# A two-block transformer kernel: the lower halves of the weight tiles on GpSimd, the key copies on VectorE

## What is computed

```python
x = first_block(x, c, ...)      # per layer: mod = silu(c) @ w_ada + b_ada; h = modulated rmsnorm(x); x += gate * rmsnorm(mixer(h) @ w_out)
for i in range(2):              # second block
    mod = silu(c_2) @ ada_w[i] + ada_b[i]
    h = modulate(rms_norm(x, norm1_g[i]), sh1, sc1)
    y = conformer_conv(h, ...) if i == 0 else hgrn2_mixer(h, ...)
    x = x + g1 * y
    h = modulate(rms_norm(x, norm2_g[i]), sh2, sc2)
    x = x + g2 * (relu(h @ w1) ** 2 @ w2)
return rms_norm(x, final_g)
```

## Time and profile before

| what | value |
|---|---|
| median of 3 runs | 2681.1 us (2674.4 to 2684.4) |
| the profiled execution | 2674.6 us, its span 2672.9 us |
| busy TensorE / VectorE / ScalarE / GpSimd | 2187.3 / 1567.2 / 918.7 / 5.3 us |
| mean granted TensorE clock | 0.91 of full |
| w_lo (L305) on VectorE | 293 instructions, 336.2 us |

### The profile page before, as it was taken

The page is one execution under the profiler, slowest core; times in us unless marked ns, Lnnn a source line. Parts: engine busy times, 40 slices in busy tenths (PEclk is TensorE's granted clock), DMA queues, the critical chain, the costliest instruction groups (busy, mean ns, idle before and its releaser), DMA issues.

```text
span 2672.9 us, 25870 instructions
## 1 busy us (share of the span) xinstructions
PE 2187.3 (82%) x9666; PEld 1641.3 (61%) x9666; DVE 1567.2 (59%) x2744; ACT 918.7 (34%) x1625; POOL 5.3 (0%) x12
## 2 busy tenths in 40 slices
PE   1898994899899665338999998777777778899997
PEld 0665563676566344216888885666666666688885
DVE  4566665666255489964655554666666674433332
ACT  2334442343322321023332233544444443422331
POOL 0000000000000000000000000000000000000000
PEclk9998997899898887669999999888888889999998
DMA  6321113333122211101555551011101111232221
GB/s 261 135 101 60 34 64 122 110 126 111 63 70 88 87 32 48 32 16 56 189 179 183 181 173 64 24 39 33 40 32 40 40 32 57 70 95 95 95 95 48
DMA packets 65723, 228.44 MB, mean 85 GB/s; under 512 B 6976, under 2 KB 9024, under 8 KB 65472
## 3 DMA queue, kind: packets, MB, share of 16 engines
q1 hardware_dynamic: 65600, 226.79, 24.8%
HBM read 224.67 MB, written 2.10 MB: 85 GB/s over the span
## 4 chain that ended last, share of the span: by engine, by line
PE 64%; DVE 22%; ACT 8%; issue 3%; DMA 2%; SPq 0%; DVEq 0%; ACTq 0%
PE bank L366 17%; PE bank L367 16%; PE bank L368 16%; DVE arena L1291 7%; PE bank L522 3%; PE bank L799 3%; PE bank L824 2%; PE bank L1405 2%; DVE arena L1488 1%; DVE arena L593 1%; DVE arena L571 1%; DMA w_raw<-weights_dram 1%; DVE h_lo L602 1%; DVE w_lo L305 1%; PE bank L812 1%
## 5 line engine op out<-in xcount | busy, mean ns | idle before, releaser
L366 PE MATMUL bank<-h_hi,w_hi 128*128 128x512 f32 (+1 forms) x1616 | 689.2, 427 | 146.7 <-DVE w_lo L305 83.6
L367 PE MATMUL bank<-h_lo,w_hi 128*128 128x512 f32 (+1 forms) x1616 | 647.0, 400 | 0.0
L368 PE MATMUL bank<-h_hi,w_lo 128*128 128x512 f32 (+1 forms) x1616 | 646.7, 400 | 0.0
L300 ACT ACTIVATE w_hi<-w_raw 128x1024 fp32r<-128x1024 f32 (+3 forms) x293 | 292.4, 998 | 565.5 <-DMA w_raw<-weights_dram 357.0
L366 PEld LDWEIGHTS bank<-h_hi,w_hi 128*128 128x128 f32 (+1 forms) x1616 | 313.6, 194 | 249.9 <-DVE w_lo L305 87.0
L305 DVE TENSOR_TENSOR w_lo<-w_raw,w_hi 128x1024 fp32r<-128x1024 f32 (+3 forms) x293 | 336.2, 1150 | 189.1 <-ACT w_hi L300 188.4
L368 PEld LDWEIGHTS bank<-h_hi,w_lo 128*128 128x128 f32 (+1 forms) x1616 | 312.7, 193 | 70.2
L367 PEld LDWEIGHTS bank<-h_lo,w_hi 128*128 128x128 f32 (+1 forms) x1616 | 315.2, 195 | 61.7 <-issue 5.7
L366 PE MATMUL bank<-a_hi_t,w_hi 128*128 128x512 f32 x512 | 202.5, 396 | 0.0
L367 PE MATMUL bank<-a_lo_t,w_hi 128*128 128x512 f32 x512 | 202.5, 396 | 0.0
L368 PE MATMUL bank<-a_hi_t,w_lo 128*128 128x512 f32 x512 | 202.5, 396 | 0.0
(11 more groups left out here) (212 smaller groups left out, 2501.0 us busy)
## 6 DMA issues: line engine op xcount, KB each, us to landing
w_raw<-weights_dram SPq DMA_DIRECT2D x261, 512.0 KB, 4.3
ada_raw<-ada_dram SPq DMA_DIRECT2D x128, 512.0 KB, 3.8
arena<-ada_dram SPq DMA_DIRECT2D x8, 1024.0 KB, 13.7
w_raw<-weights_dram SPq DMA_DIRECT2D x16, 256.0 KB, 3.8
xT<-x_dram SPq DMA_DIRECT2D x1, 2048.0 KB, 19.4
out_dram<-arena SPq DMA_DIRECT2D x1, 2048.0 KB, 7.4
tables<-tables_dram SPq DMA_DIRECT2D x1, 1408.0 KB, 21.6
w_raw<-weights_dram SPq DMA_DIRECT2D x8, 144.0 KB, 3.6
```

The lines of the kernel that those rows point to most:

```text
L300: nc.scalar.activation(WH[:, slot, 0:w], RAW[:, raw, 0:w], ACT.Copy).then_inc(w_hi_ready, 1)
L366: nc.tensor.matmul(o, WH[:, slot, cols], self.hi(k), start=(k == 0), stop=False)
L367: nc.tensor.matmul(o, WH[:, slot, cols], self.lo(k), start=False, stop=False)
L368: last = nc.tensor.matmul(o, WL[:, slot, cols], self.hi(k), start=False, stop=(k == self.K - 1))
```

## The change

`split_lo` issues its subtraction on GpSimd, and all its calls move from VectorE's program to GpSimd's. GpSimd's program has nothing else: 293 subtractions in the order of the tiles, each waiting for its `w_hi`. The places in VectorE's program where they stood, `dve_part` with them, are gone. The eight key copies go to VectorE's list (a branch that was there), where each also waits for the one before. ScalarE's, TensorE's and SP's programs are unchanged.

```diff
         def split_lo(eng, n):
             eng.wait_ge(w_hi_ready, n + 1)
-            nc.vector.tensor_tensor(WL[:, slot, 0:w], RAW[:, raw, 0:w], WH[:, slot, 0:w].bitcast(F32), ALU.subtract).then_inc(w_lo_ready, 1)
+            nc.gpsimd.tensor_tensor(WL[:, slot, 0:w], RAW[:, raw, 0:w], WH[:, slot, 0:w].bitcast(F32), ALU.subtract).then_inc(w_lo_ready, 1)
...
+            def pool_step(self, pool, i):
+                t, p = i // self.parts, i % self.parts
+                if t < self.count and p == min(1, self.parts - 1) and self.n0 + t + AHEAD < N_TILES:
+                    split_lo(pool, self.n0 + t + AHEAD)
+
             def dve_step(self, dve, i):
                 t, p = i // self.parts, i % self.parts
-                if t < self.count and p == min(1, self.parts - 1) and self.n0 + t + AHEAD < N_TILES:
-                    split_lo(dve, self.n0 + t + AHEAD)
...
-            def dve_part(self, dve, t):
-                split_lo(dve, self.n0 + t + AHEAD)
+            def pool(self, pool):
+
+                for t in range(self.count):
+                    split_lo(pool, self.n0 + t + AHEAD)
...
+        def setup_pool(pool):
             for n in range(AHEAD):
-                split_lo(dve, n)
+                split_lo(pool, n)
...
-            spread = Copies([(KV[low, h, :], Z[low, KR, :], (r1.roped, after(tm.copied, h))) for h in range(8)])
+            spread = Copies([(KV[low, h, :], Z[low, KR, :], (r1.roped, after(tm.copied, h))) for h in range(8)], on="dve")
...
-                        if self.weave and (d, l) in ((0, 5), (1, 2), (1, 5)):
-                            self.weave.dve_part(dve, ((0, 5), (1, 2), (1, 5)).index((d, l)))
+
...
         @block.vector
         def _(dve):
-            dve.sem_inc(w_lo_ready, RING)
+
             for s, i in schedule:
                 s.dve_step(dve, i)
 
         @block.gpsimd
         def _(pool):
+            pool.sem_inc(w_lo_ready, RING)
             for s, i in schedule:
                 s.pool_step(pool, i)
```

More of the change, by code:

```diff
@@ L612, in build, with __init__, pool @@
         class Do(Stage):
-            def __init__(self, pe=None, act=None, dve=None):
-                self._pe, self._act, self._dve = pe, act, dve
+            def __init__(self, pe=None, act=None, dve=None, pool=None):
+                self._pe, self._act, self._dve, self._pool = pe, act, dve, pool
+            def pool(self, e):
+                if self._pool: self._pool(e)
             def pe(self, e):
@@ L646, in build @@
         run(FirstAda())
-        run(Do(None, setup_act, setup_dve))
+        run(Do(None, setup_act, setup_dve, setup_pool))
         def second_cond_act(act):
@@ L1333, in dve @@
                     nc.vector.tensor_scalar(b, b, 2.0 ** -63, None, ALU.max).then_inc(self.mixed.sem, 1)
-                if self.woven:
-                    self.woven.dve_part(dve, 4)
         class HgrnNorm(Stage):
@@ L1454, in act, with pool @@
                     self.weave.act_part(act, 3)
+            def pool(self, pool):
+                if self.weave:
+                    self.weave.pool(pool)
             def dve(self, dve):
@@ L1526, in dve @@
                     pick(len(LEVELS))
-                if self.weave:
-                    self.weave.dve_part(dve, 3)
             def add_directions(self, dve):
```

## The result

The changed kernel takes 2717.8 us on the median (2717.3 to 2720.7, four runs) against 2680.1: ratio 1.0144, 95% interval 1.0124 to 1.0165. Forecast were 2693 us, +12. It is slower by 38, three times what was forecast, and just inside the range's upper end of 2718. A ratio here compares a kernel's runs with runs of the kernel before that were made beside them; it isn't exactly the quotient of two medians.

The account below looks back on a forecast made before the run. TensorE held 64% of the chain, VectorE setting the convolution's time and both waiting for each other in HGRN; +10 convolution, +9 HGRN, -7 y2, 0 elsewhere made +12 on 2681.1, 2693 us, range 2645 to 2718.

Parts of the forecast that it names:

- GpSimd's subtraction, taken 2.2 us, 0.9 to 2.1 us of hold: Full tile w_lo on GpSimd takes 2.2 us and holds a VectorE two-input chain 1.9 us, bounds 0.9 and 2.1.
- The two engines don't share, one waits: GpSimd reading SBUF and VectorE instructions with two SBUF inputs exclude each other; VectorE waits until about 0.2 us before GpSimd ends.
- Rivals 1 and 2: Rival 1: no exclusion, 2630 us, chance 0.12; rival 2: exclusion, but GpSimd quick (1.2 to 1.5 us), 2657 us, chance 0.14.
- rival 4: GpSimd itself is the bound; at 6 us per subtraction 128 MLP tiles cost 64 us more, 2757 us, chance 0.03.
- Convolution: 14 x 1.9 - 16.5 = +10: Convolution tap chains: 14 holds of 1.9 us less 16.5 us of removed w_lo, +10 us, bounds -4 and +13.
- y2: -7: Stretch 400 to 438 us: modulation sums 3.1 instead of 4.1 us apart, 7 us gained, bounds 3 and 9.
- Key copies: 0: Eight copies moved to VectorE cost up to 5.5 us, counted 0 because narrower w_lo leave the same stretch.
- Start: 0, bounds -3.4 and +2.3: Before the first norm: 3.4 us of w_lo removed against up to three holds of 1.9 us, taken as 0.
- HGRN: 4.65 of holds - 3 x 1.13 = +1.25 per head, +9: HGRN heads: 4.65 us of holds less three removed w_lo of 1.13 us, seven heads, +9 us, bounds -12 and +14.
- Attention and MLP: 0, bounds -5 and +15: Attention and MLP layers: VectorE loses w_lo and its wait, gets some held instructions back; net 0 us.
- Rival 3: VectorE holds reach TensorE in the attention stages, +15 us on top of the forecast's +12, 2708 us, chance 0.24.

Follow-up runs that it names:

- the runs with additional reads and writes: Kernel before, nothing removed, plus scratch GpSimd work for 16 convolution and 35 HGRN head tiles: two-input subtractions 2732.6 us; memsets 2678.9 us.
- GpSimd outside the three stages: Changed kernel with w_lo back on VectorE for the first three tiles, 16 convolution tiles and 35 inside HGRN heads: 2679.8 us, ratio 0.9998.
- GpSimd there alone: Kernel before with GpSimd making only the eight w_lo of tiles 47 to 54, key copies on VectorE: 2674.7 us, ratio 0.9990.
- the thin kernel: Kernel before with w_lo cut to 8 columns for 16 convolution and 35 HGRN head tiles, nothing new on GpSimd: 2652.6 us; with 10 additional matmuls per head 2640.6.
- the changed kernel with 10 matmuls: Changed kernel plus 10 additional matmuls in TensorE's pause in the middle of each HGRN head: 2709.4 us, ratio 1.0105.

## Why the prediction was right or wrong

- *GpSimd's subtraction, taken 2.2 us, 0.9 to 2.1 us of hold.* 2.34 to 2.41 undisturbed, 2.51 on the mean; the 512 wide form 1.27. The duration was 8% short. The estimate from the Trainium skill, "GPSIMD Engine Reference", section "Elementwise — side-by-side cycle accounting", half of its figure for 2048 elements, is 2.25 us, short as well.
- *The two engines don't share, one waits.* Right, and shown alone by the runs with additional reads and writes. What the short overlaps told held for the long operation. Rivals 1 and 2 fall, and so does rival 4: TensorE waited for GpSimd's w_lo twice, 28.4 us in all, both times in the convolution, where VectorE sets the time.
- *Convolution: 14 x 1.9 - 16.5 = +10.* Measured +10.0, with some luck. The 14 holds came to 28.0 us, 2.0 each, and without w_lo the blocks are 15.9 us shorter, which makes the +12.1 between the blocks; 2.1 us of TensorE's clock in the norm behind them, which no term had, bring it back to +10. The splits don't fall two to a block either: six fall in the first (37.1 us to the next), two in each of the next four (28.8 to 29.0), none in the last three (24.9).
- *y2: -7.* Measured -6.5 in the changed kernel, -5.6 with GpSimd outside the three stages, -5.9 with GpSimd there alone. Right in mechanism: the sums are 3.0 us apart.
- *Key copies: 0.* They cost 0.8 us where they run (tiles 34 to 40) in the changed kernel, and at tile 47 its shift is as at tile 36 (0.1 us more). The narrower w_lo that left did weigh something, as the prediction said: in the kernels that keep it the copies cost 1.1 to 1.2.
- *Start: 0, bounds -3.4 and +2.3.* Wrong: +3.9, and 2.8 to 4.0 in the four kernels with it. The step that failed is taking 0 near the middle. All three subtractions fall beside two-input work: two sums took 3.37 and 3.35 us instead of 1.22, a small addition 2.19 instead of 0.17, together +6.3, less 3.4. VectorE is through 2.95 us later; the rest up to the first norm is within the scatter there. The trace of before would have shown it: ScalarE has the first w_hi at 43.1 us, and VectorE's sums run to 45.5.
- *HGRN: 4.65 of holds - 3 x 1.13 = +1.25 per head, +9.* This is the step that made most of the miss: +25.1. The size of both terms was off, the second most. Heads are 3.9 us further apart, not 1.25. The removal was worth 1.7 us per head, not 3.39 (in the stage 8.5 us, not 23.7). The holds cost 5.6 per head, not 4.65; they fell on three instructions, as forecast, each 0.2 to 0.5 us longer than priced. The prediction subtracted busy time of an engine that stood on the chain, in a stage of which it had itself said that both engines wait for each other. The wait of 0.31 us for TensorE ahead of a select was in the profile: TensorE sets the pace of such a step, so a saving of 1.13 us on VectorE can't pass whole. The five waits of 1.70 us in the kernel without w_lo show it. One pause behind w_lo should have been followed to its next wait.
- *Attention and MLP: 0, bounds -5 and +15.* +7.0, +0.9 and +2.4 in the changed kernel, not to be told from the scatter, and +13.2 in one MLP layer of another kernel by a mere shift. Rival 3's mechanism exists; it named attention alone, where no run shows it, and the clear case is the MLP layer.
- *The sum.* Of the 26 us between +12 and +38, 16 stand in the HGRN stage and 4 in the start. Another 10 stand ahead of 928 us, where the cause stays open; against them go the 5 us by which the profiled execution of before is quicker than its median. With intervals of 0.1 to 0.2% on either side, 0.5% as the least change that can be told was too coarse.

## What to carry to other kernels

Work moved to GpSimd is not off VectorE's back: an operation with two SBUF inputs there holds every two-input one of VectorE for nearly its whole length, here 2.0 us in a chain of taps, where the same work in place costs 1.15. Here it paid only where the wait in VectorE's queue was the cost and not the subtraction, as at y2. And in a stage where two engines take turns, price a removal by what waits next, not by the time removed: here 1.7 of 3.4 us per head reached the end.

A run that hits the number of its theory proves nothing without the control: the thin kernel with the pause filled came out at 2641 as forecast, and the same matmuls in the untouched kernel showed that the reason was another.

## What the runs showed of the hardware

- A memset of 128x1024 on GpSimd takes 0.95 us and holds no tap (longest 0.755 us); a subtraction with its inputs in SBUF takes 1.91 us with an f32 result and one tensor for both inputs, 2.4 with two tensors and an fp32r result. Which of the two differences makes the 0.5 us was not tried.
- VectorE's cast L1251, with one SBUF input, is held as well: 1.59 us instead of 0.43 beside a GpSimd subtraction in the first MLP layer (at 1311 us in the changed kernel with 10 matmuls).
- The same pause of 3 us let TensorE's clock stand at 2.4 GHz in one head and fall to 1.2 in the next. Ten matmuls without a use, 2.4 us in that pause, saved 12 us in the stage of eight heads; twenty, which overran it, saved 0.5. The granted clock changed at the heads' openings too, so the pause alone doesn't account for the 12. In this kernel work without a use paid in a pause that TensorE couldn't avoid.
